# The mLSTM stage of a two-block kernel: one block matrix for the scores, gate weights multiplied by the block matrices beforehand, read-out by heads, output product by feature halves

## The reference, cut to what matters

```python
x_c = silu(dwconv(x_m, conv_w, conv_b))        # 5 taps, per feature
q = blockdiag(x_c, w_qblk)                     # 256 blocks of 4 x 4
k = blockdiag(x_c, w_kblk)
v = blockdiag(x_m, w_vblk)
gates = concatenate([q, k, v]) @ w_gate + b_gate      # 16 columns: input/forget, 2 directions, 4 heads
...
b = cumsum(logsigmoid(forget))                 # per direction and head
s = (q k^T / 16) * exp(b_t - b_s + i_s - m_t)  # masked by the direction
h = s v / max(|sum s|, exp(-m_t))
...
hn = h * rsqrt(mean(h * h) + EPS) * ml_norm    # per head
y_ml = sigmoid(z) * (hn + ml_skip * x_c)
out = (sigmoid(g_mla) * y_mla + sigmoid(g_ml) * y_ml) @ w_out
```

## Time and profile before

| | us |
|---|---|
| median of three runs (1805.71 to 1808.29) | 1806.53 |
| the profiled execution, its own time | 1807.95 |
| its span | 1806.2 |
| PE busy | 1544.8 (86%) |
| DVE / ACT / POOL busy | 490.7 / 492.4 / 581.1 |
| HBM read | 393 MB |

### The profile page before, as it was taken

How to read it: one execution, slowest core, us unless ns; L and a number is a source line. 1 busy time by engine, 2 the same in 40 slices (tenths; PEclk the granted TensorE clock), 3 DMA queues, 4 the chain that set the end, 5 groups by cost and what they waited for, 6 DMA issues and landing times. The chain is left out here.

```text
span 1806.2 us, 17176 instructions
## 1 busy us (share of the span) xinstructions
PE 1544.8 (86%) x7308; PEld 1009.5 (56%) x7308; DVE 490.7 (27%) x810; ACT 492.4 (27%) x641; POOL 581.1 (32%) x158
## 2 busy tenths in 40 slices
PE   6999999999999999999499999966877676585665
PEld 5776688877866678877487855455453131131111
DVE  1222332321322233332731338455220000000001
ACT  4254343323445254332323314422010000000000
POOL 4655277536645177643455501000000000000000
PEclk9999999999999999999799999989878878887878
DMA  6533455695544355597143460000449999999996
GB/s 235 177 120 125 140 185 168 243 332 192 186 130 129 115 187 169 180 350 279 37 136 124 146 235 17 1 13 0 153 198 423 420 422 421 422 421 421 422 422 263
DMA packets 124904, 395.36 MB, mean 219 GB/s; under 512 B 6671, under 2 KB 10564, under 8 KB 100252
## 3 DMA queue, kind: packets, MB, share of 16 engines
q1 hardware_dynamic: 122960, 388.66, 58.3%
q0 software_dynamic: 1456, 4.51, 0.7%
q10 hardware_dynamic: 412, 1.09, 0.2%
HBM read 393.18 MB, written 1.05 MB: 218 GB/s over the span
## 5 line engine op out<-in xcount | busy, mean ns | idle before, releaser
L580 POOL TENSOR_TENSOR ring_lo<-ring,ring_hi 128x2048 fp32r<-128x2048 f32 x101 | 467.8, 4636 | 374.0 <-ACT ring_hi L561 374.0
L1727 PE MATMUL psum<-ring_hi,hT_lo 128*128 128x512 f32 (+2 forms) x880 | 355.8, 404 | 22.0 <-DVE hT_lo L1978 10.7
L1729 PE MATMUL psum<-ring_hi,hT_hi 128*128 128x512 f32 (+2 forms) x880 | 345.7, 393 | 0.0
L1728 PE MATMUL psum<-ring_lo,hT_hi 128*128 128x512 f32 (+2 forms) x880 | 344.0, 391 | 0.0
L561 ACT ACTIVATE ring_hi<-ring 128x2048 fp32r<-128x2048 f32 x116 | 222.0, 1915 | 392.2 <-DMA ring<-in_w_in 123.0
L966 PE MATMUL psum<-arena 128*32 128x512 f32 x768 | 132.4, 854 | 94.7 <-DMA arena<-in_w_e_down 35.6
L1727 PEld LDWEIGHTS psum<-ring_hi,hT_lo 128*128 128x128 f32 x880 | 167.6, 190 | 64.1 <-DVE hT_lo L1978 12.1
L1729 PEld LDWEIGHTS psum<-ring_hi,hT_hi 128*128 128x128 f32 x880 | 167.5, 190 | 37.2
L1728 PEld LDWEIGHTS psum<-ring_lo,hT_hi 128*128 128x128 f32 x880 | 168.4, 191 | 33.0 <-issue 0.5
L966 PE MATMUL psum<-ring,arena 128*32 128x512 f32 x768 | 138.8, 701 | 43.5 <-DMA ring<-in_w_e_gate 18.3
L966 PEld LDWEIGHTS psum<-arena 128*32 128x32 f32 x768 | 30.6, 148 | 196.6 <-issue 80.2
(11 more groups left out here) (328 smaller groups left out, 1551.1 us busy)
## 6 DMA issues: line engine op xcount, KB each, us to landing
ring<-in_w_in SPq DMA_DIRECT2D x60, 1024.0 KB, 5.2
ring<-in_w_up SPq DMA_DIRECT2D x32, 1024.0 KB, 5.9
ring<-in_w_down SPq DMA_DIRECT2D x32, 1024.0 KB, 5.5
ring<-in_w_e_gate SPq DMA_DIRECT2D x32, 1024.0 KB, 26.8
arena<-in_w_e_gate SPq DMA_DIRECT2D x32, 1024.0 KB, 26.4
ring<-in_w_e_up SPq DMA_DIRECT2D x32, 1024.0 KB, 26.7
arena<-in_w_e_up SPq DMA_DIRECT2D x32, 1024.0 KB, 26.3
ring<-in_w_e_down SPq DMA_DIRECT2D x32, 1024.0 KB, 27.3
```

The lines of the kernel that those rows point to most:

```text
L580: eng.tensor_tensor(slot_lo(u), slot(u), slot_hi(u).bitcast(F32), ALU.subtract).then_inc(done, 1)
L1727: pe.matmul(dst, lo(k0 + k), w_hi, start=start and k == 0, stop=False)
L1728: pe.matmul(dst, hi(k0 + k), w_lo, start=False, stop=False)
L1729: last = pe.matmul(dst, hi(k0 + k), w_hi, start=False, stop=stop and k == nk - 1)
```

## The change

The scores q k^T are x_c (Wq Wk^T) x_c^T, with one block matrix for both. So the block matrices are turned and multiplied with each other, and with the gate weights, while the attention runs: six pieces of work, put by PE ahead of rounds 2, 4, ... 12 into banks 6 and 7, and copied by ACT. After the attention PE multiplies that one matrix with the latent part of `xc` (`mapped`), the gate product runs over 16 chunks (x_m and x_c), and q, k and v are no longer made with features on the partitions. ACT takes two of the four value copies and the copy of `aT`; the skip terms are multiplied in PSUM and added to `gated` by DVE, one before the logarithm, one behind the scans. z is multiplied by the norm row once, during head 0. The first three heads are normed and added to `gated` before the fourth head's result is read. `gated` is turned by feature halves, and `w_out` is applied feature half by feature half (`out_unit`), its first half before the fourth head's features are turned. The gate row of the output is spread and copied earlier. Many tiles move in the arena, and the order of the eight slots there changes. The diff, cut to its core:

```diff
+MAP_ROUNDS = (2, 4, 6, 8, 10, 12)
...
-        more_slots = [carve(first + UC * UN * i, UC, UN) for first, n in ((1536, 6), (14912, 2)) for i in range(n)]
+        more_slots = [carve(first, UC, UN) for first in (1536, 3584, 11776, 14912, 16960, 5632, 7680, 9728)]
...
-            for n in range(2):
-                src += columns(wout, UN * n, UN)
+            src += [chunks(wout[UN * kh:UN * kh + UN, UN * n:UN * n + UN]) for kh in range(2) for n in range(2)]
...
+            def turn_block(i):
+                pe.wait_ge(bd_sb, i + 1)
+                for c in range(KC):
+                    last = pe.transpose(flat[3][:, c * P:(c + 1) * P], bd[i][:, c, :], ident)
+                last.then_inc(map_full, 1)
+
+            def gates_map(i):
+
+                pe.wait_ge(rows_in, 32)
+                for c in range(KC):
+                    if i == 0:
+                        pe.matmul(psum[:, 6, c * 16:(c + 1) * 16], turned_bd[0][:, c, :], wg[:, c, :], start=True, stop=False)
+                    last = pe.matmul(psum[:, 6, c * 16:(c + 1) * 16], turned_bd[1][:, c, :], wg[:, (1 + i) * KC + c, :],
+                                     start=i == 1, stop=True)
+                last.then_inc(map_full, 1)
+
+            def scores_map():
+
+                for c in range(KC):
+                    last = pe.matmul(flat[3][:, c * P:(c + 1) * P], turned_bd[0][:, c, :], turned_bd[1][:, c, :], start=True, stop=True)
+                last.then_inc(map_full, 1)
...
+                if j in MAP_ROUNDS:
+                    i = MAP_ROUNDS.index(j)
+                    if i:
+                        pe.wait_ge(map_sb, i)
+                    if i < 2:
+                        turn_block(i)
+                    elif i == 2:
+                        gates_map(0)
+                    elif i == 3:
+                        scores_map()
+                    elif i == 4:
+                        turn_block(2)
+                    else:
+                        gates_map(1)
...
-            for i in range(6):
-                for j in range(4):
-                    last = pe.matmul(psum[32 * j:32 * j + 16, 4, :], wg[:, 4 * i + j, :], feats[4 * i + j], start=i == 0, stop=i == 5)
-            last.then_inc(gp_full, 1)
...
             values(0)
+            values(1)
+            pe.wait_ge(map_sb, 6)
+            for i in range(4):
+                if i >= 2:
+                    pe.wait_ge(xc_sb, 2 * i - 2)
+                for j in range(4):
+                    c = 4 * (i % 2) + j
+                    feat = xm[:, c, :, 2:2 + T] if i < 2 else xc[:, c, :, :]
+                    last = pe.matmul(psum[32 * j:32 * j + 32, 6, :], gate_map[:, 1 - i // 2, c, :], feat, start=i == 0, stop=i == 3)
+            last.then_inc(gp_full, 1)
+            pe.wait_ge(y2_sb, NJ2)
+            mapped(0, 2)
+            pe.wait_ge(gp_sb, 1)
+            pe.matmul(psum[0:8, 7, :], const("sel_i"), gp, start=True, stop=True)
+            pe.matmul(psum[0:8, 6, :], const("sel_f"), gp, start=True, stop=True).then_inc(gr_full, 1)
+            pe.wait_ge(vt_sb, 1)
+            mapped(1, 0)
...
+            turn_skip(0, 1)
+            pe.wait_ge(p_sb, 1)
+            turn_skip(1, 2)
+            pe.wait_ge(p_sb, 2)
+            values(2)
+            pe.wait_ge(sk_v, 2)
+            values(3)
...
-                        last = pe.matmul(flat[0][:, s * T:(s + 1) * T], qkF[:, 1, c, s * P:(s + 1) * P], qkF[:, 0, c, T:2 * T],
+                        last = pe.matmul(flat[0][:, s * T:(s + 1) * T], xc[:, c, s // 2, s % 2 * P:(s % 2 + 1) * P], pF[:, c, :],
...
+            pe.wait_ge(mix_v, 10)
+            turn_gated(0, 0)
+            pe.wait_ge(gb_sb, 1)
+            pe.wait_ge(turn_a, TURN_A + 9)
+            out_unit(0, 0)
+            pe.wait_ge(mix_v, 16)
+            turn_gated(1, 3)
+            out_unit(1, 0)
             pe.wait_ge(turn_v, TURN_V + 9)
+            out_unit(0, 1)
+            out_unit(1, 1)
...
+            value_tile(1)
+            dve.wait_ge(gp_full, 1)
+            dve.tensor_copy(gp, psum[:, 6, :]).then_inc(gp_sb, 1)
...
+            add_skip(0)
             dve.wait_ge(gr_a, 2)
...
+            add_skip(1)
...
+                if h == 0:
+                    dve.wait_ge(rows_in, 64)
+                    for t in range(TT):
+                        dve.tensor_tensor(zg[:, t, :], zg[:, t, :], ml_row, ALU.mult).then_inc(zg_sb, 1)
+                    dve.wait_ge(at_sb, 3)
+                if h == MH - 1:
+                    head_out(0, 3, 0, 6)
                 dve.wait_ge(num_full, h + 1)
...
+            head_out(3, 4, 10, 9)
...
+                if j - 1 in MAP_ROUNDS:
+                    i = MAP_ROUNDS.index(j - 1)
+                    act.wait_ge(map_full, i + 1)
+                    if i in (2, 5):
+                        act.wait_ge(map_zero, 1)
+                        act.activation(gate_map[:, i // 5, :, 0:16], psum[:, 6, 0:P].rearrange("p (c g) -> p c g", c=KC),
+                                       ACT.Copy).then_inc(map_sb, 1)
+                    else:
+                        act.activation(turned_bd[(0, 1, 0, 0, 1)[i]].rearrange("p c n -> p (c n)"), flat[3], ACT.Copy).then_inc(map_sb, 1)
...
+            for half in range(2):
+                act.wait_ge(p_full, half + 1)
+                act.activation(pF[:, 4 * half:4 * half + 4, :], flat[(2, 0)[half]].rearrange("p (c t) -> p c t", c=4), ACT.Copy)\
+                   .then_inc(p_sb, 1)
+            act.wait_ge(gr_v, 2)
             act.activation(Fb, Fb, ACT.Exp, scale=-1.0).then_inc(gr_a, 1)
...
+            pool.memset(gate_map, 0.0).then_inc(map_zero, 1)
```

More of the change, by code:

```diff
@@ L468, in build @@
         sk_v = sem("sk_v")
[L469 to L470 removed]
+        vt_a = sem("vt_a")
         rows_in = sem("rows_in")
@@ L855, in values, with mapped @@
                 last.then_inc(vt_full, 1)
-            values(0)
[L858 to L864, removed]
+            def mapped(half, db):
+                for c in range(4 * half, 4 * half + 4):
+                    last = pe.matmul(flat[db][:, c % 4 * T:(c % 4 + 1) * T], qk_map[:, c, :], xc[:, c, 1, :], start=True, stop=True)
+                last.then_inc(p_full, 1)
@@ new lines, in turn_skip @@
+            def turn_skip(t, db):
+                for c in range(KC):
+                    last = pe.transpose(flat[db][:, c * P:(c + 1) * P], skipped[:, c, t * P:(t + 1) * P], ident)
+                last.then_inc(sk_full, 1)
+            values(0)
+            values(1)
[7 more added lines that the diff above has]
+                    last = pe.matmul(psum[32 * j:32 * j + 32, 6, :], gate_map[:, 1 - i // 2, c, :], feat, start=i == 0, stop=i == 3)
@@ L865, in tensor_block2 @@
+            turn_skip(1, 2)
[3 more added lines that the diff above has]
+            values(3)
+            pe.wait_ge(gr_v, 9)
             for d in range(2):
                 for t in range(4):
[L867 to L871, removed]
+                    last = pe.transpose(psum[:, 6, 32 * d + 8 * t:32 * d + 8 * t + 8], (af, ab)[d][:, t * P:(t + 1) * P],
+                                        ident[0:8, 0:8])
@@ L912, in tensor_block2, with turn_gated, out_unit @@
                 last.then_inc(num_full, 1)
-            def spread(q, j):
-                for i in range(2):
-                    col = ident[:, 32 * (j + i):32 * (j + i) + 1].to_broadcast([P, P])
-                    last = pe.matmul(psum[:, 2 + i, :], col, modrow[:, q, :], start=True, stop=True)
-                last.then_inc(gb_full, 1)
-            pe.wait_ge(dec_a, 10 * MH)
-            spread(1, 0)
-            pe.wait_ge(h_v, 8 * MH)
-            pe.wait_ge(mix_v, 12)
-            to_features(gated)
+            def turn_gated(half, db):
+                for k in range(4):
+                    for t in range(TT):
+                        c = 4 * half + k
+                        last = pe.transpose(flat[db][:, k * T + t * P:k * T + (t + 1) * P], gated[:, t, c * P:(c + 1) * P], ident)
+                last.then_inc(turn_full, 1)
+            def out_unit(n, kh):
+                u = U_OUT + 2 * kh + n
+                unit_ready(u)
+                for t in range(TT):
+                    last = product(DB[1 + n][:, t, :], tokens(hT, t), UC * kh, u, start=kh == 0, stop=kh == 1)
+                last.then_inc(slots_free, 1)
+            pe.wait_ge(mix_v, 10)
[6 more added lines that the diff above has]
+            out_unit(1, 0)
             pe.wait_ge(turn_v, TURN_V + 9)
-            pe.wait_ge(turn_a, TURN_A + 9)
-            pe.wait_ge(gb_sb, 1)
-            for n in range(2):
-                tile_of(DB[n], hT, U_OUT + 2 * n, 0)
+            out_unit(0, 1)
+            out_unit(1, 1)
             pe.wait_ge(norm_v, 5 * 4)
@@ L1279, in weights, with head_out @@
                                              op0=ALU.mult, op1=ALU.mult).then_inc(w_v, 1)
+            def head_out(h0, h1, mv, ready):
+                heads = slice(TT * h0, TT * h1)
+                dve.wait_ge(hn_a, ready)
```

(15 more changed lines are left out.)

196 lines of the change are left out of this document (81 added, 115 removed).

## The result

The changed kernel takes 1792.26 us, the median of four runs (1790.52 to 1793.91), against 1806.12 for the kernel before, measured beside it (four runs, 1805.52 to 1808.29). The ratio is 0.991, with an interval of 0.9888 to 0.9932. It is faster by 14 us, 0.9% and clear of the noise, where 28 us were forecast, and the time lies above the range (1767 to 1789). The profiled execution took 1793.91 us, its span 1792.1.

A forecast was written before the change was run, and what follows sets the result against it. The prediction took expert-weight loads to set the end, their start set by compute ahead, mostly PE-paced in the attention. +18.7 - 25.0 - 6.2 + 0 - 15.5 = -28.0 us gave 1778.5 against 1806.53; range 1767 to 1789.

The forecast's parts named there:

- the price of the narrow products in the attention: Attention: 24 gate-weight products of 16 columns, 48 records at 0.107 us each at full clock, adding 5.1 us.
- rival 3: Attention: gaps keep PE at half clock from round 4 to 12; +36 us, 1814.5, slower than before; chance 0.05.
- The waits: Attention: PE stands still for ACT's map copies, four times 2.0 us and once 1.25, adding 9.25 us.
- the map work: Attention: transposes, block-matrix products and gate-weight products put on PE between rounds, adding 9.4 us.
- Rival 2: Attention: the clock falls to half after each of five new waits, 1.7 us each; 1787 us; chance 0.11.
- rival 4: Serial stretches after the attention give less; 1782 to 1790, say 1789 us; chance 0.12.
- From attention to gate rows: Stretch after the attention: removed feature products and a shorter gate product take 35.5 us to 10.5, -25.0.
- Gates to first weights: Gates, scans and decays up to head 0's weights: 28.1 us becomes 21.9, -6.2, ending with ACT's exps.
- Heads: Heads 0 to 2: PE sets them with the same products, so 27.6 us, unchanged.
- Output stage: Last head to output product: overlapped read-out takes 63.8 us to 48.3, -15.5, including 1.7 for one half-clock spell.
- Routing and experts: Last stages: as long as before, 44 and 446 us, so savings ahead come off the end one for one.
- Rival 5: Expert loads: all gains are lost there because the expert stream is the bound anyway; 1806.5 us; chance 0.03.

The follow-up runs named there:

- e4: Changed kernel with PE's first turning of `gated` waiting for all four heads, undoing the read-out's overlap; 1799.59 us, ratio 0.9953.
- e2: Changed kernel with the six map pieces three rounds apart instead of two, removing PE's gaps, products left 16 columns wide; 1772.47 us, ratio 0.9809.
- e3: Changed kernel with both edits: gate-map products 128 columns wide and map pieces three rounds apart; 1773.71 us, ratio 0.9814.
- e1: Changed kernel with the 24 narrow gate-map products made 128 columns wide, waits and gaps kept; 1786.14 us, ratio 0.9885.
- e8: Changed kernel with ACT's copy of the map work put ahead of the exp of its round, products still narrow; 1775.52 us, ratio 0.9812.
- e6: e5 with tile 1's skip products on DVE moved behind the first masks; 1774.29 us, ratio 0.9809.
- e7: e6 with seven unused filler products in PE's two waits ahead of the decays; 1772.8 us, ratio 0.9798.
- e9: e7 with three more unused filler products on PE around the first turning of `gated`; 1770.34 us, ratio 0.9774.
- e10: e2 run once more without an edit; 1776.93 us, ratio 0.9819.
- e5: e3 with a small Exp ahead of the two mapped copies, so its table load falls in ACT's rest; 1773.69 us, ratio 0.9805.

## Why the prediction was half right

The profiled execution came out at 1793.91 for 1779.95, 14.0 us more. By stage: attention 11.2 (85.25 for 18.7 on 55.33), gate rows 0.6, first weights 0.5, output 0.3, routing 0.5, rest 1.8, and 1.0 less ahead of the attention.

**The step that failed** is the price of the narrow products in the attention: "In the attention the clock is 1.00, so 0.107 each". The clock was 1.00 with the work that stood there, and the step put other work in. I took the clock of the stage before the edit for the clock of the edit, and bounded only the price of a record, not that of all the rounds behind it. What the runs showed: with 128 columns in the same places and the same gaps the attention takes 73.84 us, the forecast 74.0 almost to the digit; with these gaps in place the narrow columns make 11.4 more (8.1 in e4), and without the gaps 3.2 (e2 against e3).

The trace before held a warning next to the row that was used. Behind the four records at 1.00 in the earlier trace rows the same stream of the router's narrow products goes on at half clock, PE being busy, and the clock is still 0.50 ten microseconds later:

```profile
1311.00:1311.50 0.50, 0.50 (x5) 0.58 1.05 442
1312.00:1314.00 2.00, 2.00 (x11) 0.50 1.01 426
1318.00:1321.00 3.00, 2.39 (x5) 0.50 1.02 426
```

PE had rested 2.41 us just before these products, so the stretch can't tell the columns from the rest. But it has work on both sides of a rest of 2.41 us and the clock down for some 10, which the prediction, in its argument against rival 3, said this trace did not have.

**The waits** were right in place, cause and number: four of 1.70 or 1.71 for 2.0, one of 0.95 for 1.25. The 1.5 us too much went against some 1.4 us too little for the map work: PE's busy time is 54.89 before and 65.73 in e1, 10.8 more where 9.4 were put. That the total met the forecast was so in part the luck of two errors of opposite sign. (Between e1 and e3 the gaps are worth 8.8 and the map work 9.7, which makes both errors smaller.) That the gaps need not be there at all, since ACT's rest of 2.1 us ahead of its exp is free, was named among the bounds and confirmed by e8.

**Rival 2** was nearest in kind to what came (1787; rival 4's 1789 was nearer in number, but its stages kept to the forecast), with the wrong cause. It hung the fall on each of the five waits; e1 has all five and no fall. **Rival 3** (half clock from round 4 to 12, slower than before) came true in part, as the spells are long and begin at pieces with a gap, at a loss of 11.4 us where it needed 28. The Trainium skill (TensorE: Matmul & The Clock Gate, section HAM oscillation — how this bites in real kernels) tells of waits for DMAs, longer than these gaps, that bring the clock down each time. Of narrow products it says nothing there. By gaps alone e1 and the changed kernel should have had the same clock; they had 1.00 and 0.86.

**From attention to gate rows**: 11.08 for 10.5. The four gate products ran abreast (32 records in 3.68, for 3.44 and the 3.73 of the earlier trace rows), and nothing but the input's tiles stood ahead of them (3.74). **Gates to first weights**: 22.40 for 21.9. The Exp's load lay behind the second mapped copy, as told, each step about 0.8 late (the copy at 14.0 after the attention's end for 13.2, the logarithm at 17.9 for 17.1). The Trainium skill (ScalarE: Activation LUTs, section What ACT_TABLE_LOAD costs) has a drain of 1.38 us beside the load; here the load began 0.02 us after the copy's end and the Exp 0.02 after the load's, so this trace doesn't agree, and the forecast did well to leave it out. Only the end was put down wrongly: the first weights waited 3.88 us for PE's scores (L917), not for ACT's exps, which were through at 1205.8; e6 shows that DVE's skip products did not count, and e7, with its full clock, that PE's did. In the changed kernel the clock was 0.50 from 1200 to 1204 us, and PE made them from 1200.4 to 1206.3.

**Heads** 27.55 for 27.6. **Output stage** 48.64 for 48.3: e4 takes the overlap away and loses 7.1, and e9, without a spell of half clock, takes 1.7 less, which is what the forecast put in for it. **Routing and experts** nearly kept their length, 44.69 and 464.89: what was saved ahead came off the end in every kernel of the table, less 1.4 to 3.4 us by which the last stretch was longer than before (464.47 to 466.55 for 463.10). Rival 5 did not come.

**What stays open.** Why the second narrow piece is followed by half clock where a gap stands before it (changed kernel and e4) and not where none does (e2, e8, e10): the first piece is twice as long, and the two differ in what stands ahead. A rest and narrow work behind it may add up to what the longer piece does alone; that is a guess. A gap at one piece alone, or the first piece cut in two, was not tried. Nor is it shown why the last stretch is longer in every changed kernel.

## What to carry to other kernels

The clock in a stage belongs to the work that is in it: when an edit puts short products into a stretch of wide ones, price the rounds behind them at half clock as well, and look whether wider products cost the same time, as here 128 columns for 16. Where two engines take turns, put the copy that the other waits for in the rest of the first, not behind its own work. In an unavoidable rest of PE of some microseconds a few products without use kept the clock at 1.00 here; those that outlasted the wait cost 1.2 us of what they gained.

## What was not expected of the hardware

- A product of 128x16 and one of 128x128 take the same time at full clock, 0.38 and 0.39 us for two records, yet the clock fell behind the first kind in all five profiles that have it (the changed kernel, e2, e4, e8, e10), and in none of the six attentions with the second (e1, e3, e5, e6, e7, e9).
- The loss is larger with a gap of 1.7 us ahead of the narrow products: 11.4 us lost in the changed kernel, and 8.1 in e4 with the same attention, against 3.2 in e2 and e10.
- Gaps of 1.7 us at every second round cost nothing of the clock with wide work around them (1.00 over 73.8 us in e1).
- Seven products without use shortened their stage by 1.8 us (21.37 to 19.59), three more the output stage by 3.0 (49.88 to 46.91), or by 1.7 against the 48.64 of the changed kernel.
